# Feed-forward blocks of the second half: multiply first, apply the norm's root at the PSUM exit

## What is computed

```python
for i in range(DEPTH_2):                       # 4 layers
    x = x + mix                                # kind i % 3: diff attention, hgrn2, sgu
    x = x + mem_cross_attention(rmsnorm(x, norm_cross[i]), mem_n, ...)
    x = x + swiglu(rmsnorm(x, norm_ffn[i]), ffn_w_gu[i], ffn_w_down[i])

def rmsnorm(x, g):
    y = xf * lax.rsqrt(jnp.mean(xf * xf, axis=-1, keepdims=True) + EPS)
    return (y * g.astype(jnp.float32)).astype(x.dtype)

def swiglu(h, w_gu, w_down):                   # 1024 -> 2 x 2816 -> 1024
    gate, up = jnp.split(h @ w_gu, 2, axis=-1)
    return (jax.nn.silu(gate) * up) @ w_down
```

## Time and profile before

| | us |
|---|---|
| median of 3 runs | 3210.6 (3210.41 to 3212.27) |
| the profiled execution | 3214.22 |
| its span, first to last instruction | 3212.4 |
| PE busy | 2900.8 (90%) |
| PE weight loads busy | 2798.9 (87%) |
| DVE busy | 1845.9 (57%) |
| ACT busy | 1318.2 (41%) |
| POOL busy | 0.7 |

### The profile page before, as it was taken

The page is one execution under the profiler, slowest core; times in us unless marked ns, Lnnn a source line. Parts: engine busy times, 40 slices in busy tenths (PEclk is TensorE's granted clock), DMA queues, the critical chain, the costliest instruction groups (busy, mean ns, idle before and its releaser), DMA issues.

```text
span 3212.4 us, 53330 instructions
## 1 busy us (share of the span) xinstructions
PE 2900.8 (90%) x22527; PEld 2798.9 (87%) x22527; DVE 1845.9 (57%) x2554; ACT 1318.2 (41%) x1548; POOL 0.7 (0%) x5
## 2 busy tenths in 40 slices
PE   2899969999997899969999978999989999979998
PEld 2799949999995799949899977999989999859998
DVE  5787766778758554555454563545544445544444
ACT  2333524344353443444443513444434444444433
POOL 0000000000000000000000000000000000000000
PEclk6899969999998899979999998999989999989999
DMA  5897506868852155515255513345544355523353
GB/s 183 255 303 249 164 7 225 292 229 291 288 186 92 53 197 195 191 47 171 77 200 182 184 48 110 119 158 177 191 143 144 122 193 184 171 66 131 132 183 105
DMA packets 458657, 533.07 MB, mean 166 GB/s; under 512 B 9863, under 2 KB 434937, under 8 KB 458489
## 3 DMA queue, kind: packets, MB, share of 16 engines
q1 hardware_dynamic: 458489, 530.76, 50.3%
HBM read 528.10 MB, written 2.62 MB: 165 GB/s over the span
## 4 chain that ended last, share of the span: by engine, by line
PE 82%; DVE 10%; ACT 3%; DMA 2%; issue 2%; SPq 1%; DVEq 0%; ACTq 0%
PE ps L1681 14%; PE ps L1534 14%; PE ps L1535 13%; PE ps L1536 13%; PE ps L1551 13%; PE ps L1641 2%; PE ps L1581 2%; PE ps L1580 2%; PE ps L1579 2%; PE ps L1741 2%; PE ps L1712 1%; DVE work L1281 1%; DMA bias_rows<-raw 1%; DVE wlo L983 1%; DMA work<-in_ada_w 1%
## 5 line engine op out<-in xcount | busy, mean ns | idle before, releaser
L983 DVE TENSOR_TENSOR wlo<-raw,whi 128x2048 fp32r<-128x2048 f32 (+1 forms) x514 | 977.3, 1920 | 685.1 <-ACT whi L668 685.0
L668 ACT ACTIVATE whi<-raw 128x2048 fp32r<-128x2048 f32 (+1 forms) x514 | 825.5, 1612 | 641.5 <-PE ps L1536 402.6
L1534 PE MATMUL ps<-hhi,whi 128*128 128x256 f32 x3344 | 958.6, 287 | 43.7 <-issue 9.9
L1535 PE MATMUL ps<-hlo,whi 128*128 128x256 f32 x3344 | 954.3, 285 | 0.0
L1536 PE MATMUL ps<-hhi,wlo 128*128 128x256 f32 x3344 | 954.0, 285 | 0.0
L1534 PEld LDWEIGHTS ps<-hhi,whi 128*128 128x128 f32 x3344 | 650.6, 195 | 52.4 <-issue 51.8
L1535 PEld LDWEIGHTS ps<-hlo,whi 128*128 128x128 f32 x3344 | 650.6, 195 | 0.0
L1536 PEld LDWEIGHTS ps<-hhi,wlo 128*128 128x128 f32 x3344 | 650.2, 194 | 0.0
L1681 PE MATMUL ps<-ghi,whi 128*128 128x256 f32 x1280 | 363.0, 284 | 3.3 <-DVE wlo L983 3.3
L1681 PE MATMUL ps<-glo,whi 128*128 128x256 f32 x1280 | 363.0, 284 | 0.0
L1681 PE MATMUL ps<-ghi,wlo 128*128 128x256 f32 x1280 | 362.9, 284 | 0.0
(11 more groups left out here) (227 smaller groups left out, 3397.9 us busy)
## 6 DMA issues: line engine op xcount, KB each, us to landing
raw<-in_ffn_w_in SPq DMA_DIRECT2D x88, 1024.0 KB, 8.1
raw<-in_ffn_w_gu SPq DMA_DIRECT2D x88, 1024.0 KB, 5.0
work<-in_ada_w SPq DMA_DIRECT2D x72, 1024.0 KB, 8.7
raw<-in_ffn_w_out SPq DMA_DIRECT2D x88, 512.0 KB, 5.7
raw<-in_ffn_w_down SPq DMA_DIRECT2D x88, 512.0 KB, 5.4
raw<-in_ca_w_kv SPq DMA_DIRECT2D x32, 1024.0 KB, 5.4
raw<-in_mix_w_in SPq DMA_DIRECT2D x24, 1024.0 KB, 6.0
raw<-in_da_w_in SPq DMA_DIRECT2D x24, 1024.0 KB, 5.3
```

Of the source, the lines that this page charges most:

```text
L668: f(whi[:, s, 0:size], raw[:, s, 0:size], ACT.Copy).then_inc(hi_done[s], 1)
L983: tt(wlo[:, s, 0:size], raw[:, s, 0:size], whi[:, s, 0:size].bitcast(F32), ALU.subtract).then_inc(lo_done[s], 1)
L1534: mm(dst, wh, xh, start=first, stop=False)
L1535: mm(dst, wh, xl, start=False, stop=False)
```

## The change

In the four ffn stages of the second half:

- The input of the products is `x` times gain, not times root, in tiles of its own, `fhi` and `flo`. ACT writes `fhi` (Copy with the gain as per-partition scale) ahead of each pair's square. DVE writes `flo` from `x`, gain and `fhi` (`low_of_x`); for pairs 0 to 2 this stands in `outp`, behind the addition to `x` of the pair after, and for pair 3 in the norm.
- DVE adds the squares of the four pairs into one (`add_up`, three additions of 128x512), so that PE sums 2 products instead of 8. PE does this after A(0) instead of ahead of it.
- DVE multiplies bank A by the root into `silu_a`, ACT takes silu in place, DVE multiplies bank B by the root into `product` and that by `silu_a`: three multiplications in place of one.
- For the early norm of the cross attention and for the changed norms, ACT's `ahead` stands behind the squares instead of before them.
- SBUF is found for `fhi` and `flo` (16 KB per partition): the scratch for software transfers is cut to 512 bytes, and `vec` is packed more tightly.

The counting of norms that scale `x` (`turn`) is kept apart from that of all norms. The core of the diff:

```diff
         vec = sb("vec", [P, 380])
+        fhi = sb("fhi", [P, KT, S], F32R)
+        flo = sb("flo", [P, KT, S], F32R)
...
 # ACT, norm
                 for p in range(4):
                     act.wait_ge(*st.ready[p])
+                    if st.defer is not None:
+                        name, at = st.gain
+                        for k in (2 * p, 2 * p + 1):
+                            f(fhi[:, k, :], x[:, k, :], ACT.Copy, scale=col(name, at + k)).then_inc(q["norm_hi"], 1)
                     f(norm_x[:, 2 * p:2 * p + 2, :], x[:, 2 * p:2 * p + 2, :], ACT.Square).then_inc(q["norm_sq"], 1)
+                if st.early or st.defer is not None:
+                    ahead(st.pos)
...
-                if st.source == "final":
+                if st.source == "final" or st.defer is not None:
                     return
 # ACT, ffn
+                    if st.defer is not None:
+                        act.wait_ge(read[A], st.reads[A] + j + 1)
+                        f(silu_a, silu_a, ACT.Silu).then_inc(q["ffn_silu"], 1)
...
                     act.wait_ge(read[B], st.reads[B] + j + 1)
+                    if st.defer is not None:
+                        act.wait_ge(q["ffn_prod"], STEPS * st.defer + j + 1)
 # DVE, norm
+            def add_up(st):
+                for p in range(1, 4 if st.add is not None else 1):
+                    dve.wait_ge(q["norm_sq"], 4 * st.i + p + 1)
+                    if p > 1:
+                        dve.wait_ge(q["norm_add"], 3 * st.add + p - 1)
+                    tt(norm_x[:, 0:2, :], norm_x[:, 0:2, :], norm_x[:, 2 * p:2 * p + 2, :], ALU.add)\
+                        .then_inc(q["norm_add"], 1)
+            def low_of_x(st, p):
+                name, at = st.gain
+                for k in (2 * p, 2 * p + 1):
+                    dve.wait_ge(q["norm_hi"], 8 * st.i + k + 1)
+                    stt(flo[:, k, :], x[:, k, :], col(name, at + k), fhi[:, k, :].bitcast(F32), ALU.mult, ALU.subtract)\
+                        .then_inc(q["norm_lo"], 1)
...
+                if st.defer is not None:
+                    low_of_x(st, 3)
+                    add_up(st)
+                    ahead(st.pos)
+                    return
 # DVE, ffn
-                    ahead(pb)
+                    ahead(pb if st.defer is None else pa)
+                    if st.defer is not None:
+                        dve.wait_ge(used[A], st.uses[A] + j + 1)
+                        if j == 0:
+                            dve.wait_ge(q["norm_rs"], st.late.i + 1)
+                        n = STEPS * st.defer + j
+                        if n:
+                            dve.wait_ge(q["ffn_prod"], n)
+                        root = rstd[:, 1:2, :].broadcast_to([P, 2, S])
+                        tt(silu_a, rows2(ps[:, A, :]), root, ALU.mult).then_inc(read[A], 1)
+                        ahead(pb)
+                        dve.wait_ge(used[B], st.uses[B] + j + 1)
+                        dve.wait_ge(q["ffn_lo"], lo0 + j)
+                        tt(product, rows2(ps[:, B, :]), root, ALU.mult).then_inc(read[B], 1)
+                        dve.wait_ge(read[B], st.reads[B] + j + 1)
+                        dve.wait_ge(q["ffn_silu"], n + 1)
+                        tt(product, product, silu_a, ALU.mult).then_inc(q["ffn_prod"], 1)
+                        ahead(o1 if j else pb + 1, AHEAD if j < STEPS - 1 else 2)
+                        dve.wait_ge(q["ffn_hi"], lo0 + j + 1)
+                        dve.wait_ge(q["ffn_prod"], n + 1)
+                        tt(glo[:, :, :], product, ghi[:, :, :].bitcast(F32), ALU.subtract).then_inc(q["ffn_lo"], 1)
+                        continue
 # DVE, outp
                     m.then_inc(read[u.slot], 1)
+                    if st.then and n:
+                        low_of_x(st.then, n - 1)
 # PE, norm
-                for p in range(4):
+                if st.add is not None:
+                    pe.wait_ge(q["norm_add"], 3 * st.add + 3)
+                    for k in range(2):
+                        o = mm(ps[:, st.bank, 0:S], ones, norm_x[:, k, :], start=k == 0, stop=k == 1)
+                for p in range(4 if st.add is None else 0):
 # PE, ffn
                 ab(A, 0, first=True)
+                if st.defer is not None:
+                    norm(st.late, True)
                 ab(B, 0)
 # kernel
-    nc = bacc.Bacc("TRN2", target_bir_lowering=False, num_devices=1)
+    nc = bacc.Bacc("TRN2", target_bir_lowering=False, num_devices=1, dynamic_dma_scratch_size=512)
```

More of the change, by code:

```diff
@@ L137, in __init__ @@
                  uses=None, ada=None, last=None, gn=None, heads=None, masked=None, pairs=None, tree=None,
-                 rope=None, j=None, layer=None, n=None, h=None, early=False, late=None):
+                 rope=None, j=None, layer=None, n=None, h=None, early=False, late=None, add=None, defer=None, turn=None, then=None):
         self.kind = kind
@@ L146, in __init__ @@
         self.j, self.layer, self.n, self.h, self.early, self.late = j, layer, n, h, early, late
+        self.add, self.defer, self.turn, self.then = add, defer, turn, then
 class Unit:
@@ L227, in build @@
         glo = sb("glo", [P, 2, S], F32R)
+        fhi = sb("fhi", [P, KT, S], F32R)
+        flo = sb("flo", [P, KT, S], F32R)
         con = sb("con", [P, N_RESIDENT])
-        vec = sb("vec", [P, 4, P])
+        vec = sb("vec", [P, 380])
+        VEC = (0, 128, 236, 308)
         mods = sb("mods", [P, 2 * N_MOD * KT])
@@ L253, in col @@
             tile, at = ROWS[name]
-            return vec[:, tile, at + i:at + i + n]
+            return vec[:, VEC[tile] + at + i:VEC[tile] + at + i + n]
         def work(at, *dims):
@@ L347, in build @@
         stages = plan.stages
-        tally = dict.fromkeys("norm modnorm ffn gn heads masked pairs tree rope project out diff".split(), 0)
+        tally = dict.fromkeys("add defer norm modnorm ffn gn heads masked pairs tree rope project out diff".split(), 0)
         def take(name, n=1):
@@ L444, in build @@
             ready = out_project(a["ca_w_o_2"][i])
-            norm("norm_ffn_2", i, ready, 4)
+            out_stage = stages[-1]
+            out_stage.then = norm("norm_ffn_2", i, ready, 4)
+            out_stage.then.defer, out_stage.then.add = take("defer"), take("add")
             ready = ffn(a["ffn_w_gu_2"][i], a["ffn_w_down_2"][i])
+            stages[-1].defer, stages[-1].late = out_stage.then.defer, out_stage.then
         norm("norm_final_2", 0, ready, 2, source="final")
@@ L453, in build @@
             st.h = current
-        n_norms = sum(st.kind == "norm" for st in stages)
+        scaled_norms = [st for st in stages if st.kind == "norm" and st.defer is None]
+        for turn, st in enumerate(scaled_norms):
+            st.turn = turn
+        n_norms = len(scaled_norms)
         n_stream = len(plan.stream)
@@ L701, in norm @@
                 log_exp_tables()
-                if st.early:
-                    ahead(st.pos)
                 if 8 * i > 0:
@@ L719, in norm @@
                 for k in range(KT):
-                    act.wait_ge(q["norm_t"], 8 * i + k + 1)
+                    act.wait_ge(q["norm_t"], 8 * st.turn + k + 1)
                     if st.mod is None:
@@ L734, in ffn @@
                     ahead(pa)
[L735 to L738, removed]
+                    if st.defer is not None:
+                        act.wait_ge(read[A], st.reads[A] + j + 1)
+                        f(silu_a, silu_a, ACT.Silu).then_inc(q["ffn_silu"], 1)
+                    else:
+                        act.wait_ge(used[A], st.uses[A] + j + 1)
+                        if st.reads[B] + j > 0:
+                            act.wait_ge(read[B], st.reads[B] + j)
+                        f(silu_a, ps[:, A, :], ACT.Silu).then_inc(read[A], 1)
                     ahead(pb)
@@ L994, in prologue @@
                 for t, n in enumerate((128, 105, 72, 72)):
-                    m = v.tensor_copy(vec[:, t, 0:n], ps[:, 0, 128 * t:128 * t + n])
+                    m = v.tensor_copy(vec[:, VEC[t]:VEC[t] + n], ps[:, 0, 128 * t:128 * t + n])
                 pro("vec", m)
@@ L1076, in ada_columns @@
                     if a0 < a1:
-                        m = tt(mods[:, a0:a1], ps[:, bank, a0:a1], vec[:, 2 + l, a0 - 72 * l:a1 - 72 * l], ALU.add)
+                        m = tt(mods[:, a0:a1], ps[:, bank, a0:a1], vec[:, VEC[2 + l] + a0 - 72 * l:VEC[2 + l] + a1 - 72 * l], ALU.add)
                 m.then_inc(q["ada_col"], 1)
@@ L1096, in norm @@
                     sc = 72 * l + 8 * (3 * n + 1)
-                    dve.wait_ge(q["norm_t"], 8 * i)
+                    dve.wait_ge(q["norm_t"], 8 * st.turn)
                     stt(gain[:, :], mods[:, sc:sc + 8], 1.0, col(name, at, KT), ALU.add, ALU.mult)\
@@ L1543, in h_parts, with both @@
                 return (mhi, mlo) if src == "mem" else (hhi, hlo)
-            def both(slot, th, tl, h):
+            def both(slot, th, tl, h, src=(hhi, hlo)):
+                hi, lo = src
                 for k in range(KT):
```

(11 more changed lines are left out.)

3 lines of the change are left out of this document (2 added, 1 removed).

## The result

| | before | after |
|---|---|---|
| median | 3210.6 (5 runs, 3209.28 to 3212.27) | 3195.87 (5 runs, 3191.92 to 3196.24) |
| profiled execution, span | 3214.22, 3212.4 | 3196.24, 3194.5 |
| DVE busy | 1845.9 (57%) | 1901.1 (60%) |

The ratio is 0.995, with a 95% interval from 0.9935 to 0.9965: 14.7 us less by these medians, where 21.4 was forecast. The forecast was 3189.2 in a range of 3181 to 3198. With later runs of both kernels on one chip the medians were 3195.62 against 3211.64, and 3193.18 against 3211.76: 16.0 and 18.6 less.

A forecast was written before the change was run, and what follows sets the result against it. PE was taken as the bound, with 82% of the chain. Each ffn's start would go from 30.94 to 25.60 us, 5.34 less, 21.4 for four layers, off the median 3210.6: 3189.2, range 3181 to 3198.

The forecast's parts named there:

- border: From output projection to outputs of the ffn's step 0: 30.94 us before, 25.60 after, 5.34 less for each layer.
- A(0) at once and at full clock: Start of each ffn: first product begins as the output projection ends, PE not idle, 5.76 us instead of 7.48.
- sums of 0.87: Behind A(0): PE sums 2 of 8 products of squares, 0.87 us instead of 3.47.
- the additions hidden: DVE's three additions of squares under A(0): done near T + 5.0, wanted at 5.76, 0.8 us to spare.
- no clock lost at the stall: At the wait ahead of A(1): the sum took no clock loss there, though PE idles for 1.34 us.
- no cost in the loop: DVE's two more multiplications in each of 44 steps cost nothing, hidden by 6.8 us of cover and the wait of `ghi`.
- The new stall: Ahead of A(1), PE waits 1.34 us for log, exp, table load, silu and splits; ahead of B(1), 0.35.
- I take the saving off it: Final sum: 21.4 us for four layers subtracted from the median of the runs shown, 3210.6, giving 3189.2.
- Rival 1: Stall ahead of A(1) also costs the clock, 1.72 us each time: 3196.1; 12%.
- Rival 2: ACT's table load ahead of silu costs more than its row: 3194.3, or 3194.7 by the skill's drain; 10%.
- Rivals 3, 4 and 5: No stalls, 3182.4, 6%; loop slower by late DVE work, 3250, 4%; early start of A(0) or sums fails, 3207, 4%.
- The moved `whi` of the early norm: Cross attention's early norm: one `whi` of 1.91 us behind four squares, taken as nothing; bounds 7.6 us either way.

The follow-up runs named there:

- e3: Changed kernel with the splits of A(1) placed ahead of log and exp and those of B(1) ahead of `ghi` in step 0; 3185.08, ratio 0.9914.
- e6: Kernel before, with 20 matmuls of no use in the idle gaps of the four ffn norms; 3209.36, ratio 0.9993.
- e8: Changed kernel without DVE's three additions of squares, so PE sums eight products again behind A(0); 3199.82, ratio 0.9964.
- e9: Kernel of e3 with 14 matmuls of no use between B(0) and A(1), 1.68 us; 3192.36, ratio 0.9938.
- e11: Kernel of e3 run again with no edit, for a second trace; 3182.51, ratio 0.9907.
- e4: Changed kernel with 20 matmuls of no use in each of nine idle norm gaps; 3184.32, ratio 0.9912.
- e5: Changed kernel with 20 matmuls of no use in three gaps only, the mixer norms of layers 1, 2 and 3; 3189.36, ratio 0.9934.
- e7: Kernel before, with 20 matmuls of no use in the mixer norms of layers 1, 2 and 3; 3209.94, ratio 0.9992.
- e10: Changed kernel with the edits of e3 and e4 together; 3174.37, ratio 0.9885.

## Why the prediction was right, and where it was off

- **Direction and border.** Right. The forecast of the border was 5.34 us for each layer and the traces have 5.02, 20.0 for four by the stretches (1169.9 less 1149.9). A(0) at once and at full clock, sums of 0.87, the additions hidden, no clock lost at the stall, no cost in the loop: each row is where it was put.
- **The new stall.** It was found from rows of the kernel before and has the cause that was given; e3 removed it by moving the splits. Its size was short by a term: 1.34 and 0.35 us were forecast. Measured were waits of 1.39 and 0.18 us and then a first matmul of 0.36 instead of 0.12 each time. The earlier trace rows may have shown a sign of it, 0.28 at 2131.74. The second wait was shorter than forecast, since PE came to it 0.3 us later; the two restarts, 0.48 us, were not in the sum. Together 2.05 against 1.69.
- **The step that failed** is "I take the saving off it", the median: the sum had no term for the clock outside the border. It counted 1.72 us of clock at each ffn's start (e6 showed 1.48 of clock and 0.24 of restart, which the changed kernel saves as well), and treated the other gaps of 2.5 us as fixed. They are not: in the first trace of before one of the three mixer norms of layers 1 to 3 had lost the clock, in the changed kernel all three. The mixer stretches, in which the change has next to nothing, grew from 728.2 and 730.2 us to 731.9 to 732.9, by 3.3 us on the mean. Of this the first runs behind the three norms give 2.4, and the rest lies inside the mixers. So 20.0 of borders less 3.3 leaves 16.7, between the savings by medians of 14.7, 16.0 and 18.6. That the range took in 3195.87 is in part luck: its upper end was built from the new stall, not from other gaps. What is left between two traces of one kernel is outside the last four layers: the last outputs of the first half begin anywhere from 1288.3 to 1293.6 us in the traces of the two kernels.
- **Rival 1** (the stall costs the clock, 3196.1) met the time nearly to the microsecond (3195.87), by luck, and is wrong as a mechanism: the clock is 1.00 through the stall and behind it. The clock was lost, but at other gaps.
- **Rival 2.** Silu starts 0.01 us behind the table load (2107.44 + 1.28, 2108.73). The drain that the Trainium skill ("ScalarE: Activation LUTs", section "What ACT_TABLE_LOAD costs") adds to a load is not seen behind it, nor ahead of it (exp ends at 2107.42), and the trace decides.
- **Rivals 3, 4 and 5.** The stalls did come; the loop is at 17.28 us with DVE at 9.68; A(0) did start early.
- The moved `whi` of the early norm cost nothing: from that norm's sums to the query products 32.25 us pass in the changed kernel (2001.08 to 2033.33) and 32.26 in the one before.

Does the change bring the losses at the three norms about? Counts alone do not say: nine of nine in the changed kernel and three of three in e6 were lost, three of six before, but e3, e8, e9 and e11 lost seven of twelve, and they keep the clock at the ffn's start as well. The places in the table above say that the change acts through time. Its shorter borders shift all that follows, and in the changed kernel the gaps of layers 2 and 3 began at nearly the same places in three traces, 0.88 to 0.96 and 0.14 to 0.19, all in the losing part. In the kernel before several began close to the edges of that part (0.36, 0.40, 0.43, 0.82), and they fell either way. That this kernel's stages put them there is luck, and other lengths give other patterns (e3, e8, e9). This is a sorting of traces, not an experiment: no run shifted a gap by a chosen fraction of a microsecond, and why layer 1's place varies from run to run is open.

## To carry to other kernels

When a wait is removed ahead of a product, list what the first weights behind it wait for: a split or a table load that the old wait had hidden is the next one in line, and it can often be moved ahead at no cost (here 8.0 us more in the borders). Where gaps keep or lose TensorE's clock by the moment at which they come, judge an edit by the stretches that it touches as well as by the total, since the clock of unchanged stages moved the total by up to 6 us. Matmuls of no use in such a gap saved 11.3 us in nine gaps, where the change itself saved 16, and together with moved splits they made the fastest version.

## What the runs showed of the hardware

- The same idle gap of PE, 2.5 us behind 3.47 us of full-f32 sums, kept the 2.4 GHz level in one trace and fell to 1.2 GHz in the next of the same kernel, at 1.3 to 1.5 us a time. Which of the two went by the moment at which the gap began, in 51 gaps of 51. Twenty f32r matmuls in the gap (2.4 us) kept the clock in all 28 gaps of e4, e5, e6, e7 and e10 that had them.
- Idle gaps of 1.4 us, behind products, kept the clock in all four layers of the six traces that have them (the changed kernel's three, e4, e5, e8).
- At both stalls of the changed kernel, of 1.39 and of 0.18 us, the first f32r matmul behind the wait takes 0.36 us of PE's chain, and the following ones 0.12.
- A table load of 1.28 us is followed by the next activation after 0.01 us, for silu as for the square.
